# A hybrid decoder step on one core: attention over pairs of heads with row halves, token placing by one-hot products, and a last stage in two VectorE passes

## The reference

```python
def masked_softmax(s, mask):
    p = jax.nn.softmax(jnp.where(mask, s, NEG), axis=-1)
    return jnp.where(mask, p, 0.0)

def attend_shared(q, k, v, mask):
    s = jnp.einsum('bthgd,bkhd->bthgk', q, k, ...) * HEAD_DIM ** -0.5
    p = masked_softmax(s, mask)
    return jnp.einsum('bthgk,bkhd->bthgd', p.astype(v.dtype), v), p
```

```python
    slot_tok = jnp.full((cap,), n, jnp.int32).at[dest].set(tok_sorted).reshape(n_blocks, MOE_BLOCK)
    slot_w = jnp.zeros((cap,), jnp.float32).at[dest].set(w_sorted).reshape(n_blocks, MOE_BLOCK)
    def expert_block(i, acc):
        y = swiglu(h_pad[slot_tok[i]], w_gate[block_e[i]], w_up[block_e[i]], w_down[block_e[i]])
        return acc.at[slot_tok[i]].add(y * slot_w[i][:, None])
```

## Time and profile before

| | us |
|---|---|
| median of 3 runs (lowest, highest) | 2868.99 (2868.76, 2873.95) |
| profiled execution | 2866.09 |
| its span in the profile | 2864.4 |
| mean granted TensorE clock | 0.87 |

### The profile page before, as it was taken

One profiled execution on the slowest core, in us unless ns is written; L12 is line 12 of the kernel. 1 busy time (PEld: TensorE's weight loads), 2 busy tenths in 40 slices (PEclk: granted clock), 3 DMA queues, 4 the chain that ended last, 5 costly groups with the idle time before them and its releaser, 6 DMA issues. The chain is left out here.

```text
span 2864.4 us, 39048 instructions
## 1 busy us (share of the span) xinstructions
PE 2216.0 (77%) x11359; PEld 1644.9 (57%) x11359; DVE 978.0 (34%) x2216; ACT 426.4 (15%) x881; POOL 523.9 (18%) x753
## 2 busy tenths in 40 slices
PE   7999975527999578998222599940999999999970
PEld 4766745407999456776122344410777777777750
DVE  3344416650000344443388256570111111111113
ACT  1111110000000144444000001000111111111111
POOL 0000001002331143222122000025122222222213
PEclk9999976656999589999566699975999999999995
DMA  6011022018884200000413311101899999999973
GB/s 229 29 48 42 24 76 56 29 43 236 284 285 153 89 8 8 4 4 4 188 62 125 113 63 69 52 11 56 315 356 358 351 353 360 358 346 354 358 227 133
DMA packets 167995, 448.21 MB, mean 156 GB/s; under 512 B 32972, under 2 KB 103541, under 8 KB 141337
## 3 DMA queue, kind: packets, MB, share of 16 engines
q1 hardware_dynamic: 108176, 327.50, 30.3%
q0 software_dynamic: 27744, 94.12, 12.4%
q10 hardware_dynamic: 32000, 25.70, 2.9%
HBM read 391.84 MB, written 69.95 MB: 161 GB/s over the span
## 5 line engine op out<-in xcount | busy, mean ns | idle before, releaser
L888 PE MATMUL ph<-pages,weight_room 128*128 128x128 f32 (+1 forms) x2176 | 260.0, 284 | 22.2 <-DMA pages<-o_kv_cmp_prompt 22.2
L888 PEld LDWEIGHTS ph<-pages,weight_room 128*128 128x128 f32 x2176 | 258.4, 201 | 23.3 <-issue 22.8
L2196 PE MATMUL e_pG<-e_gate,e_xT 128*128 128x256 f32 x1072 | 244.9, 382 | 1.3 <-ACT e_xT L2233 0.8
L2196 PE MATMUL e_pG<-e_up,e_xT 128*128 128x256 f32 x1072 | 242.3, 379 | 0.0
L2210 PE MATMUL e_pY<-e_down,e_hT 128*128 128x512 f32 x536 | 241.2, 593 | 0.5 <-ACT e_hT L2250 0.5
L2196 PEld LDWEIGHTS e_pG<-e_up,e_xT 128*128 128x128 f32 x1072 | 203.7, 190 | 27.7
L2196 PEld LDWEIGHTS e_pG<-e_gate,e_xT 128*128 128x128 f32 x1072 | 200.5, 192 | 26.7 <-ACT e_xT L2233 1.2
L2148 POOL DMA_INDIRECT s_acc<-e_y,add_rows x67 | 106.4, 1589 | 572.2 <-ACT e_y L2267 566.6
L2276 DVE TENSOR_TENSOR e_h<-e_silu,e_pG 128x256 f32<-128x256 f32 x67 | 28.2, 421 | 435.5 <-ACT e_silu L2246 435.5
L2210 PEld LDWEIGHTS e_pY<-e_down,e_hT 128*128 128x128 f32 x536 | 96.8, 190 | 96.9 <-issue 96.8
L1166 PE MATMUL att_pO<-v_rows,probsT 128*128 128x128 f32 x1056 | 143.8, 282 | 0.0
(11 more groups left out here) (456 smaller groups left out, 2992.7 us busy)
## 6 DMA issues: line engine op xcount, KB each, us to landing
e_gate<-i_exp_gate SPq DMA_DIRECT2D x67, 1024.0 KB, 6.8
e_up<-i_exp_up SPq DMA_DIRECT2D x67, 1024.0 KB, 8.8
e_down<-i_exp_down SPq DMA_DIRECT2D x67, 1024.0 KB, 7.8
pages<-i_cache_kv_cmp ACTq DMA_DIRECT2D x192, 128.0 KB, 6.4
pages<-i_cache_kv_cmp SPq DMA_DIRECT2D x192, 128.0 KB, 5.5
pages<-i_cache_kv_cmp POOLq DMA_DIRECT2D x128, 128.0 KB, 5.2
w_in_sb<-i_w_in SPq DMA_DIRECT2D x3, 2048.0 KB, 15.9
weight_room<-i_x SPq DMA_DIRECT2D x8, 512.0 KB
```

Of the source, the lines that this page charges most:

```text
L888: mm = nc.tensor.matmul(ph[h][:, kv * P:kv * P + n], w1[:, kv, c], moving(c, kv), start=(c == 0), stop=(c == EC - 1))
L2196: mm = nc.tensor.matmul(pG[u][:, at:at + FE], xT[u][:, c], w[u][:, c], start=(c == 0), stop=(c == DC - 1))
```

## The change

**project**: ScalarE's copy of the turned queries into `qrT` multiplies by -1/8 for the prompt's tiles. **attend**: the zero-padded copies on GpSimd go; a scores matmul reads 64 rows of `qrT` and of the keys, and the two heads of a pair write two pairs of banks. Scores come out negated, so that the softmax's maximum is a minimum; VectorE adds a mask for all keys, writes the sum to `probs` and takes the minimum in one instruction; the exponential runs in place. The copy of the turned probabilities is split: ScalarE takes the first 512 columns, VectorE the others. The order is written out for 64 steps s (t, c, branch), both heads a step. **route**: instead of scatter and reload, VectorE writes for each of 54 choices a one-hot of the slot in the block and two rows that hold token and weight at the block's place; TensorE sums their products into `r_pG`. **experts**: the first pair, a loop over 7, and six groups of 8 pairs, each behind one branch. **finish**: ScalarE makes the sums of tiles 2, 4 and 6, VectorE the statistics of the others, then for each tile two passes that subtract, multiply and add; GpSimd keeps operations of one column. **build**: the clearing of semaphores and its barrier stand between `sample` and `route`.

```diff
 # project
-                nc.scalar.copy(k.qrT[:, :, at], pT[:, 1, :].rearrange(...)[:, :, 0:R])
+                    nc.scalar.activation(k.qrT[:, :, at], turned, ACT.Copy, scale=-SCALE)
...
 # attend
+            sp.wait_ge(masks_ready, 1)
+            for dst, src in ((mask_sel[:, SEQ - P:SEQ], "mask_diag"), (mask_win[:, WK - P:WK], "mask_diag"),
+                             (mask_win[:, 0:P], "mask_neg"), (visn[:], "cmp_mask"), (vis[:], "cmp_vis"),
...
-                for gr in range(2):
-                    rows = slice(gr * 64, gr * 64 + 64)
-                    nc.gpsimd.tensor_tensor(qst[gr][rows, :], k.qrT[rows, ...], scale[rows, :], ALU.mult)
-                g.drain().then_inc(staged, 1)
...
-                    mm = nc.tensor.matmul(pS[j % 2][:, i // 512, 0:w], qst[gr][:], K[br][:, k0 + i:k0 + i + w], ...)
+                    for gr in range(2):
+                        if i == 0 and s:
+                            pe.wait_ge(masked[gr], s)
+                        rows = slice(gr * 64, gr * 64 + 64)
+                        mm = nc.tensor.matmul(pS[gr][:, i // 512, 0:w], k.qrT[rows, c, t * P:(t + 1) * P],
+                                              K[br][rows, k0 + i:k0 + i + w], start=True, stop=True)
...
+            for s in range(NP_ + 2):
+                if s < NP_:
+                    scores(s, 0, 512)
+                if 1 <= s <= NP_:
+                    turn(s - 1, 0)
+                if s >= 2:
+                    values(s - 2, 1)
+                if s < NP_:
+                    scores(s, 512, SEQ)
+                if 1 <= s <= NP_:
+                    turn(s - 1, 1)
+                    values(s - 1, 0)
...
-                nc.vector.tensor_tensor(S[:, n - P:n], S[:, n - P:n], diag[:], ALU.add)
-                nc.vector.tensor_reduce(nm[:, j:j + 1], S[:, 0:n], AX.X, ALU.max, negate=True).then_inc(max_ready, 1)
+                nc.vector.tensor_tensor_reduce(Sm[s % 2][gr][:, 0:n], pS[gr][:].rearrange("p a b -> p (a b)")[:, 0:n], mask,
+                                               1.0, -NEG, ALU.add, ALU.min, nm[:, at:at + 1])
+                v.drain().then_inc(masked[gr], 1)
...
+                nc.scalar.copy(PT[gr][:, 0:n // P].rearrange("p a b -> p (a b)"), pT[:, 0, 0:n]).then_inc(copied_a[gr], 1)
...
 # route
-                    g.indirect_dma_start(d["slot_rows"], bass.IndirectOffsetOnAxis(dest[0:R, t, c:c + 1], 0),
-                                         choice[0:R, t, c], None).then_inc(scattered, 16)
...
+                    mm = nc.tensor.matmul(pG[:, 0:2 * NBLK], at_slot[t % 2][0:R, c],
+                                          in_block[t % 2][0:R, c].rearrange("p a n -> p (a n)"), ...)
...
+                    nc.vector.tensor_scalar(at_slot[t % 2][0:R, c], io128[0:R], slotf[0:R, t, c:c + 1], None, ALU.is_equal)
+                    for a, value in enumerate((tokf[0:R, t:t + 1], chosen_w[0:R, t, c:c + 1])):
+                        last = nc.vector.tensor_scalar(in_block[t % 2][0:R, c, a], io128[0:R, 0:NBLK], blkf[0:R, t, c:c + 1],
+                                                       value, ALU.is_equal, ALU.mult)
...
 # experts
+        def pairs_of_blocks(eng, nb, body):
+            body(0, True)
+            with eng.Fori(1, GROUP) as i:
+                body(i, False)
+            with eng.Fori(1, NBLK // 2 // GROUP) as group:
+                with eng.If(nb > group * (2 * GROUP)):
+                    with eng.Fori(0, GROUP) as j:
+                        body(group * GROUP + j, False)
...
 # finish
+        by_act = (2, 4, 6)
+        ready_order = (0, 1, 2, 3, 5, 4, 7, 8, 6)
...
-                if t == 0:
+                if t == 2:
                     sp.dma_start(gain[:], bcast(d["ln2_g"], [P, D])).then_inc(consts, 16)
...
-                nc.gpsimd.tensor_tensor(out[0:R, t], out[0:R, t], bias[0:R], ALU.add).then_inc(out_ready, 1)
...
+                nc.vector.scalar_tensor_tensor(out=out[0:R, t], in0=acc[0:R, t], scalar=mv[0:R, t, 0:1], in1=gain[0:R],
+                                               op0=ALU.subtract if t in by_dve else ALU.add, op1=ALU.mult)
+                v.drain()
+                nc.vector.scalar_tensor_tensor(out=out[0:R, t], in0=out[0:R, t], scalar=rstd[0:R, t:t + 1], in1=bias[0:R],
+                                               op0=ALU.mult, op1=ALU.add)
```

More of the change, by code:

```diff
@@ L1042, in keys, with wide_until @@
             return (t + 1) * P - first_key(t, br)
[L1045 to L1062, removed]
+        def wide_until(s):
+            return sum(keys(t, br) > 512 for t, c, br in pairs[0:s + 1])
         @block.sync
         def _(sp):
[L1066 to L1068 removed]
+            sp.wait_ge(masks_ready, 1)
+            for dst, src in ((mask_sel[:, SEQ - P:SEQ], "mask_diag"), (mask_win[:, WK - P:WK], "mask_diag"),
+                             (mask_win[:, 0:P], "mask_neg"), (visn[:], "cmp_mask"), (vis[:], "cmp_vis"),
+                             (spread[:], "spread16"), (slot[:], "slot_mask")):
+                sp.dma_start(dst, d[src]).then_inc(consts, 16)
             for v_sb, rows in zip(V, (d["kv_sel_prompt"], d["kv_win_all"][0:SEQ])):
@@ L1132, in _, with scores @@
                              stop=True).then_inc(c_turned, 1)
-            def scores(t, c, j):
-                br, gr = branch(j)
+            def scores(s, low, high):
+                t, c, br = pairs[s]
                 k0, n = first_key(t, br), keys(t, br)
-                for i in range(0, n, 512):
+                for i in range(low, min(n, high), 512):
                     w = min(512, n - i)
-                    mm = nc.tensor.matmul(pS[j % 2][:, i // 512, 0:w], qst[gr][:], K[br][:, k0 + i:k0 + i + w],
-                                          start=True, stop=True)
-                mm.then_inc(s_done, 1)
@@ new lines, in turn @@
+            def turn(s, gr):
+                n = keys(pairs[s][0], pairs[s][2])
+                pe.wait_ge(exped[gr], s + 1)
+                before = s if gr else s - 1
+                if before >= 0:
+                    pe.wait_ge(copied_a[1 - gr], before + 1)
+                    if wide_until(before):
+                        pe.wait_ge(copied_b[1 - gr], wide_until(before))
+                for i in range(n // P):
+                    mm = nc.tensor.transpose(pT[:, i // 4, (i % 4) * P:(i % 4 + 1) * P], Sm[s % 2][gr][:, i * P:(i + 1) * P],
@@ L2120, in _, with pair @@
             load_gate_up(1, 1)
-            with sp.Fori(0, NBLK // 2) as i:
+            def pair(i, first):
                 for u in range(2):
@@ L2217, in _, with pair @@
             turn_hidden(0, 0)
-            with pe.Fori(0, NBLK // 2) as i:
+            def pair(i, first):
                 for u in range(2):
@@ L2255, in _, with pair @@
             hidden_turned(0, 0)
-            with act.Fori(0, NBLK // 2) as i:
+            def pair(i, first):
                 for u in range(2):
```

406 lines of the change are left out of this document (217 added, 189 removed).

## The result

The changed kernel takes 2775.95 us (median of 4 runs, 2774.75 to 2779.42) where the kernel before takes 2868.88: a ratio of 0.9674, 95% interval 0.9657 to 0.9691. Faster, as forecast, and inside the range; the forecast of 2760 was 16 us too low. The profiled execution has a span of 2773.0 us, 91.4 less than before.

The account below looks back on a forecast made before the run. Attention was paced by TensorE, though with gaps; afterwards a loop through VectorE would bound it. 2866.1 - 71 (attention) - 11 (placing) - 0.7 (clearing) - 15 (empty end) - 8 (last stage) = 2760 us, range 2700 to 2815.

Parts of the forecast that it names:

- The loop: Attention: a loop through VectorE's masking passes and TensorE's order sets the time, 313 us against 386.
- a visit to the halves: Attention, TensorE: going between 64-row and 128-row matmuls costs 0.1 us a change, 192 changes.
- VectorE's part of the narrow steps: Attention, up to 4 tiles of keys: handover, add_out, two masking passes; 0.2 + 0.36 + 1.62 + 0.05 us for 4.
- the forecast's terms: Attention: scores, changes, turn, values, handover, VectorE's passes and release add to a step, 5.4 us for 5 tiles of keys.
- The third rival: Attention: the halves don't pay, a change costs 0.3 us and halves run one after the other; 2814 us, chance 0.2.
- one sign of being wrong: Attention: score pairs of a step that start one after the other would show the forecast wrong; no size given.
- The first rival: Attention: TensorE is the bound, the loop takes 252 + 3 us and the kernel 2702; chance 0.07.
- Placing: Placing of tokens: one-hots and TensorE products replace scatters, ending at 1976.6 against 1987.4: -11 us, from -22 to +1.
- Empty end: End of the expert loop: fewer empty pairs to walk, some 6.6 us, 2795 against 2810.3: -15, bounds -13 and -18.
- Experts: Busy part of the expert loop: each engine meets a group's branch four times, 0 to +3 us, taken as 0.
- Last stage: Last stage: two VectorE passes a tile, 23.8 us for 18, stage 45.9 against 54: -8, ends -4 and -11.

Follow-up runs that it names:

- mask_twice: after with the second head's masking pass made twice in each of the 64 steps: 2847.63 us.
- mask_first: after with high scores right behind low on TensorE, ScalarE in narrow order throughout, VectorE's masking passes ahead of the sums: 2721.88 us.
- after: The changed kernel itself, against the kernel before: 2775.95 us, ratio 0.9674.
- padded_first: mask_first with scores over 128 rows again, from zero-padded queries that GpSimd copies: 2759.83 us.
- more_visits: mask_first with the high scores issued behind the first turn, one more visit to the halves in each of 32 steps: 2748.57 us.
- edges: after with expert groups of 7 pairs, gain and bias loaded after tile 1, VectorE's passes of tiles 0 to 3 between the statistics: 2769.94 us.
- padded: after with scores over 128 rows again, from zero-padded queries that GpSimd copies: 2770.90 us.

## Why the prediction was right, and where it was off

*The loop.* Right: the changed attention is not bound by TensorE's work but by a loop through the masking passes and the order on two engines, and an added microsecond in that loop is at least a microsecond of time (mask_twice). It is why TensorE's work, which took 272 us once the orders were turned round (mask_first), took 327 here.

*Two terms were too small: a visit to the halves, and VectorE's part of the narrow steps.* I took 0.1 us for each of 192 changes between halves and whole rows, 0.2 a visit. The step of 5 tiles against the forecast's terms, from the second head's low scores on: those 1.04 against 0.96, turn 0.60 against 0.55, values 1.21 against 1.22, high scores 0.43 against 0.22, and VectorE's part 2.34 against 2.41: 5.62 against 5.36. TensorE's part, with the two visits of the step, is 0.33 dearer, some 0.16 a visit. A visit so costs 0.36 in after, 0.34 by padded_first, 0.28 in more_visits' rows.

96 visits at 0.16 make 15 us, and the loop missed its forecast by 14, but that this fits is partly luck. By the visits alone the narrow steps, with one each, would miss half of what the wide ones miss; they miss as much (4 tiles of keys: 4.9 us for a forecast of 4.6; 5 tiles: 5.6 for 5.4). A narrow step, with 4 tiles of keys, from one of the second head's masking passes to the next:

```profile
1089.13 0.69 DVE L1193 CUSTOM_DVE_ANT_0 probs<-att_pS,mask_sel 128x512 f32<-128x512 f32 x1 [0.23 <-issue]
...
1090.97 0.66 PE L1121 MATMUL att_pT<-ident,probs 128*128 128x128 f32 x4
1091.46 1.06 PE L1134 MATMUL att_pO<-v_rows,probsT 128*128 128x128 f32 x8
...
1092.56 0.28 DVE L1212 SCALAR_TENSOR_TENSOR nsa_y<-att_pO,gate_over_sum,nsa_y 128x64 f32<-128x64 f32 x1 [2.25 <-PE att_pO L1134]
1093.07 0.69 DVE L1193 CUSTOM_DVE_ANT_0 probs<-att_pS,mask_sel 128x512 f32<-128x512 f32 x1 [0.23 <-issue]
...
1094.00 0.69 DVE L1193 CUSTOM_DVE_ANT_0 probs<-att_pS,mask_sel 128x512 f32<-128x512 f32 x1 [0.23 <-issue]
```

That is 4.87 us; the forecast's terms add up to 4.52, put down as 4.6. 0.27 of the 0.35 lie on VectorE: 0.51 from the sum to the first masking pass, where 0.36 was put, and 0.93 from there to the second, where 0.81 was. The pass itself is not what is dearer; VectorE stands idle for 0.23 us ahead of each, for which the forecast had only the 0.08 of the sum's drain. In the wide steps, where a copy stands between the passes, VectorE's part came out as priced, and there the visits are what is missing.

The earlier trace rows could not price a visit: they hold one way out of the halves and no way in, behind passes of 4 columns, at a granted clock of 0.50. Nor is the 0.22 us from pair to pair a price of the halves. In the kernel before, matmuls of 8 columns on all 128 rows took as long at the same clock, 72 of them 15.51 us (the windows give the clock of both stretches):

```profile
380.75 15.51 PE L292 MATMUL pX<-weight_room,w_in_sb 128*128 128x8 f32 x72
...
381.00:396.00 15.00, 15.00 (x72) 15.00 (x72) 0.00 (x0) 0.00 (x0) 0.00 (x0) 0.50 0.00 1
1371.00:1374.50 3.50, 3.47 (x32) 3.47 (x32) 0.00 (x0) 0.00 (x0) 0.00 (x0) 0.50 0.98 332
```

The third rival (0.3 a change and halves one after the other, 2814) had the direction; a change costs some 0.17. The Trainium skill, "TensorEngine Tiling (Array Packing)", Key Properties, says that a change of tiling mode drains TensorE; the rows here agree that a visit has a price of its own, and give it. And one sign of being wrong that the prediction named did come: in after the two heads' scores start 0.2 to 0.9 us apart, for the second head waits for its masking pass. The loop carries only one head's scores, so that this cost little; with both heads free (mask_first) they start together and run side by side.

*The first rival* (TensorE the bound, 2702) is what the kernel became when the orders were turned round: 272 us in the loop where I had put 255.

*Placing.* -13.7 to VectorE's end (1859.50 to 1920.82, 61.3 us, against 75.0), forecast -11: one-hots start 0.20, 0.25 and 0.25 us apart, 4.15 a tile and not 4.5. Another 5.1 come from the gap before the experts, which held the clearing; 3.9 of them are paid ahead of the routing stage, where the engines now stand empty for 5.9 us instead of 2.0.

```profile
1877.64 0.29 DVE L2051 TENSOR_SCALAR slot_oh<-slot_in_block,dest_in_block 128x128 f32<-128x128 f32 x1
1877.84 0.33 DVE L2053 TENSOR_SCALAR block_oh<-slot_in_block,dest_block,tok_f 128x112 f32<-128x112 f32 x1
1878.09 0.34 DVE L2053 TENSOR_SCALAR block_oh<-slot_in_block,dest_block,choice_weight 128x112 f32<-128x112 f32 x1
1878.34 0.28 DVE L2051 TENSOR_SCALAR slot_oh<-slot_in_block,dest_in_block 128x128 f32<-128x128 f32 x1
...
1920.55 0.27 DVE L2075 TENSOR_TENSOR slot_token<-vacant,r_pG 128x112 int32<-128x112 f32 x1
```

*Empty end.* -13.9 for -15: the drain is the same 3.41 us, the walk took 8.1 us from the end of the last add and not 6.6. *Experts.* +0.9, inside the 0 to 3; from the first matmul to the last add it is 777.8 us before, 778.7 in after, 778.2 in mask_first and 776.8 in edges, so that the groups' branches cost nothing that stands out of the scatter. *Last stage.* -6.7 for -8: passes of 1.28 us start 1.36 to 1.41 apart, 24.8 us for eighteen instead of 23.8, and the first starts 19.4 us into the stage and not 18.6; the last store and end took 3.1, not 3.5.

```profile
2745.10 1.28 DVE L2437 SCALAR_TENSOR_TENSOR f_out<-f_acc,mv,ln_g_sb 128x1024 f32<-128x1024 f32 x1 [0.21 <-issue]
2745.32 1.46 POOL L2386 TENSOR_TENSOR rstd<-rstd,mhalf 8x1 f32<-8x1 f32 x1
2746.46 1.28 DVE L2440 SCALAR_TENSOR_TENSOR f_out<-f_out,rstd,ln_b_sb 128x1024 f32<-128x1024 f32 x1
...
2769.94 0.33 SPq L2370 DMA_DIRECT2D o_y_prompt<-f_out  x1
```

## What to carry to other kernels

An engine's busy column does not say that it is the bound: find the wait that closes the loop, and ask what of each engine's order stands ahead of it; here new orders gave 54 us with the same instructions, 31 of them by an order of VectorE alone, while TensorE's and ScalarE's alone cost 11. Before an order is changed, list what is queued behind the instruction that will wait: the copy behind the masking pass cost 53 us. Before a row prices something, look up its clock, and whether an operation of the same size takes as long without the thing to be priced. And when a count times a price gives the miss, check it where the count differs: steps with one visit and with two missed alike.

## What the runs showed of the hardware

A visit of TensorE to matmuls on 64 rows, between matmuls on 128, cost 0.28 to 0.36 us beside its columns, at 2.4 GHz. A pass of 512 columns on 64 rows that came first took 0.53 us, one behind it 0.43; the two heads' passes on the two halves started 0.01 us apart (mask_first). At 1.2 GHz matmuls of 8 columns on all rows came 0.22 us apart, as did pairs of 4 columns on the halves.

GpSimd's operation of one column (L2405) took 0.55 us before VectorE's passes of two memory operands began, and 1.58 beside them:

```profile
2742.49 0.55 POOL L2405 TENSOR_TENSOR rstd<-mv,mhalf 128x1 f32<-128x1 f32 x1
...
2749.35 1.58 POOL L2405 TENSOR_TENSOR rstd<-mv,mhalf 128x1 f32<-128x1 f32 x1
```

The granted clock of the loop's first 28 us, as a share of 2.4 GHz, differed between kernels: 0.56 in after, 0.63 in mask_first, 0.94 in padded, 0.88 in padded_first (0.5 is the lower level, 1.2 GHz). The first query tile took 27.8 us in after and 23.9 in padded; how much of that is the clock was not separated. After and then padded:

```profile
979.00:1007.00 28.00, 26.42 (x92) 18.49 (x93) 10.29 (x53) 12.80 (x53) 13.30 (x36) 0.56 0.00 1
...
979.00:1007.00 28.00, 22.97 (x111) 16.20 (x112) 12.36 (x60) 14.65 (x59) 18.40 (x49) 0.94 0.03 11
```

TensorE's busy time there was the lower one where the clock was higher; what decides the clock no run here isolates.
